# Dilated attention with keys stored by residue and queries copied contiguous

## The reference

```
PATTERNS = ((128, 1), (512, 4), (2048, 16))          # window, dilation d
q, k, v, g_attn, c_h, c_b, c_c, g_conv = split(rmsnorm(x) @ w_in)
q, k = rope(q), rope(k)
for window, d in PATTERNS:
    # positions regrouped by residue mod d: d sequences of 2048 / d positions
    # in blocks of 128: a query sees the keys of its own block and of the one before,
    # at distances 0 .. 128 in its sequence
    s = q . k / 8, masked outside the window
    m = max(s); p = exp(s - m); den = sum(p)
    o_d, lse_d = (p / den) @ v, m + log(den)
w_d = softmax over the three lse_d
attn = sum_d w_d * o_d * silu(g_attn)
x = x + rmsnorm(concat(attn, conv) @ w_out)
```

## Time and profile before

| | |
|---|---|
| median of 3 runs (lowest to highest) | 2533.55 us (2531.64 to 2534.88) |
| the profiled execution, its span | 2524.11 us, 2522.6 us |
| busy in the span: PE, PEld | 2282.0 us (90%), 2068.9 us (82%) |
| DVE, ACT, POOL | 1381.9 us (55%), 819.0 us (32%), 689.7 us (27%) |
| PE matmul L1835 of qkkA, qkqA, x288 | 131.3 us, 456 ns each |
| DVE mask pass L1901, x576 | 185.9 us, 360 ns each |
| DVE rest L1907, x288 | 164.9 us, 572 ns each |
| first and last scores of the dilated stage | 1802.0, 2284.4 us |

### The profile page before, as it was taken

How to read it: one execution, slowest core, us unless ns; L and a number is a source line. 1 busy time by engine, 2 the same in 40 slices (tenths; PEclk the granted TensorE clock), 3 DMA queues, 4 the chain that set the end, 5 groups by cost and what they waited for, 6 DMA issues and landing times.

```text
span 2522.6 us, 42770 instructions
## 1 busy us (share of the span) xinstructions
PE 2282.0 (90%) x16422; PEld 2068.9 (82%) x16422; DVE 1381.9 (55%) x3442; ACT 819.0 (32%) x1910; POOL 689.7 (27%) x658
## 2 busy tenths in 40 slices
PE   6999799988588899599999999999698999996898
PEld 5988799888577688499888888989698888895776
DVE  6513777946699444662365533031386777785321
ACT  4411111111578010242122211000376776774111
POOL 0012021135241798101121211111105444553222
PEclk9999899999899899899999999999898998998999
DMA  4341231124850332332455531211569866964443
GB/s 151 99 111 59 75 96 30 47 83 140 207 145 27 126 123 94 125 110 77 135 184 169 172 126 55 63 36 62 148 146 200 201 166 152 217 181 148 157 140 107
DMA packets 283803, 308.23 MB, mean 122 GB/s; under 512 B 38112, under 2 KB 221280, under 8 KB 280144
## 3 DMA queue, kind: packets, MB, share of 16 engines
q1 hardware_dynamic: 281776, 299.46, 41.4%
q0 software_dynamic: 1680, 5.51, 0.7%
q10 hardware_dynamic: 144, 0.52, 0.1%
HBM read 186.95 MB, written 105.89 MB: 116 GB/s over the span
## 4 chain that ended last, share of the span: by engine, by line
PE 68%; DMA 9%; DVE 9%; issue 5%; POOL 4%; SPq 3%; ACT 1%; ACTq 0%; POOLq 0%; DVEq 0%
PE bank L165 54%; PE bank L1835 4%; DVE acc L694 3%; PE bank L1836 3%; DMA cm<-scr_part 3%; PE bank L1846 3%; PE bank L1864 2%; DMA woR<-in_w_out 2%; PE bank L364 1%; SPq L1955 1%; POOL wol L1201 1%; POOL yo L2113 1%; SPq L1957 1%; PE bank L1269 0%; DMA w2r<-in_w_in 0%
## 5 line engine op out<-in xcount | busy, mean ns | idle before, releaser
L165 PE MATMUL bank<-w1h,xh 128*128 128x256 f32 (+1 forms) x896 | 259.7, 290 | 14.9 <-DVE s1st L684 14.9
L165 PE MATMUL bank<-w1l,xh 128*128 128x256 f32 (+1 forms) x896 | 255.6, 285 | 0.0
L165 PE MATMUL bank<-w1h,xl 128*128 128x256 f32 (+1 forms) x896 | 255.2, 285 | 0.0
L165 PE MATMUL bank<-xh,w2h 128*128 128x512 f32 x640 | 249.0, 389 | 0.0
L165 PE MATMUL bank<-xl,w2h 128*128 128x512 f32 x640 | 249.0, 389 | 0.0
L165 PE MATMUL bank<-xh,w2l 128*128 128x512 f32 x640 | 249.0, 389 | 0.0
L165 PE MATMUL bank<-w2h,xh 128*128 128x256 f32 x768 | 218.5, 284 | 10.3 <-issue 9.0
L165 PE MATMUL bank<-w2l,xh 128*128 128x256 f32 x768 | 217.9, 284 | 0.0
L165 PE MATMUL bank<-w2h,xl 128*128 128x256 f32 x768 | 217.9, 284 | 0.0
L1901 DVE CUSTOM_DVE_ANT_0 s2m<-bank,mask 128x256 f32<-128x256 f32 (+1 forms) x576 | 185.9, 360 | 46.1 <-PE bank L1836 44.5
L694 DVE SCALAR_TENSOR_TENSOR acc<-ain,cw,acc 128x512 f32<-128x512 f32 x240 | 200.1, 835 | 8.9 <-ACT acc L651 1.8
(11 more groups left out here) (273 smaller groups left out, 6017.2 us busy)
## 6 DMA issues: line engine op xcount, KB each, us to landing
scr_part<-ob SPq DMA_DIRECT2D x48, 264.0 KB, 2.8
cm<-scr_part SPq DMA_DIRECT2D x48, 264.0 KB, 4.8
v<-scr_v SPq DMA_DIRECT2D x12, 1040.0 KB, 7.5
w2r<-in_w_in SPq DMA_DIRECT2D x12, 1024.0 KB, 6.8
qr<-qf SPq DMA_DIRECT2D x192, 64.0 KB, 2.0
ax<-in_x SPq DMA_DIRECT2D x16, 512.0 KB, 6.1
xr<-in_x SPq DMA_DIRECT2D x16, 512.0 KB, 4.5
bx<-scr_x SPq DMA_DIRECT2D x16, 512.0 KB, 6.2
```

The source lines that it names most:

```text
L165: ins = nc.tensor.matmul(dst, x, y, start=k == 0 and m == 0, stop=k == n - 1 and m == 2)
```

## The change

1. **Keys by residue.** The rope stage's two split instructions for the 24 key tiles read positions with a stride of 16 and write them in order of their residue mod 16: within each block of 512 positions, 16 runs of 32. The DRAM arrays and the loads stay as they are, only the order of the columns differs.
2. **Queries.** The pair's queries lie in `qn`, both heads in one tile, by position. For d = 1 TensorE still takes them as a contiguous slice. For d = 4 and 16 a new GpSimd instruction ("queries", 96 in all) copies the queries of two units and both heads, 512 columns, to one of six `qs` tiles, contiguous. It is put eight steps ahead of its first unit, ahead of the step's other work, and waits for the pair's loads and for the scores of the unit that used the tile last. The scores of these units wait for it (`g_qs`).
3. **Keys in the matmul** (`keys_of`). For d = 16 runs of 32 columns, for d = 4 runs of 32 in another order, for d = 1 runs of 8. So the scores of d = 4 and 1 leave TensorE with their columns by residue.
4. **The mask pass** puts them back: it reads the bank in its order, reads the mask and writes `s2m` with a stride of 4 elements for d = 4 and of 16 for d = 1. For d = 16 it is unchanged.

```diff
@@ -1426,11 +1426,18 @@
             act_split(N - 2)
             act_split(N - 1)
 
+        def stored(m, x):
+
+            return x[:].rearrange("p (r a) -> p r a", r=16) if tiles[m]["n"] >= 3 else x[:]
+
+        def taken(m, x):
+            return x[:].rearrange("p (a r) -> p r a", r=16) if tiles[m]["n"] >= 3 else x[:]
+
         def act_split(m):
             act.wait_ge(*d_rp.at(3 * m + 3))
             act.wait_ge(*h_out[m % 2].at(16 * (m // 2)))
             act.wait_ge(*d_ql.at(m - 1))
-            nc.scalar.activation(hbuf[m % 2][:], qf[m % 3][:], ACT.Copy).then_inc(*a_qh.up())
+            nc.scalar.activation(stored(m, hbuf[m % 2]), taken(m, qf[m % 3]), ACT.Copy).then_inc(*a_qh.up())
 
         def dve_program():
             for m in range(N):
@@ -1445,7 +1452,7 @@
                 nc.vector.tensor_tensor(q[:], q[:], r[:], ALU.add).then_inc(*d_rp.up())
                 dve.wait_ge(*a_qh.at(m + 1))
                 dve.wait_ge(*l_out[m % 2].at(16 * (m // 2)))
-                nc.vector.scalar_tensor_tensor(lbuf[m % 2][:], q[:], 1.0, f(hbuf[m % 2][:]), ALU.mult, ALU.subtract).then_inc(*d_ql.up())
+                nc.vector.scalar_tensor_tensor(stored(m, lbuf[m % 2]), taken(m, q), 1.0, f(stored(m, hbuf[m % 2])), ALU.mult, ALU.subtract).then_inc(*d_ql.up())
 
         def pool_program():
             for n in range(6):
@@ -1609,7 +1616,8 @@
         ce, cd = sbs("ce", 2, [128, 4, 4, 2], F32, late_scope), sbs("cd", 2, [128, 4, 4, 2], F32, late_scope)
         wp = OutWeights("wp", late_scope, A["w_out_2"], 256, 2, None, None)
         scope = stack().__enter__()
-        qk = [[sb(f"qk{n}{i}", [128, S], FR, scope) for n in ("qA", "qB", "kA", "kB", "lA", "lB")] for i in range(2)]
+        qn, qs = sbs("qn", 2, [128, 2, S], FR, scope), sbs("qs", 6, [128, 2, 2, 128], FR, scope)
+        kk = [[sb(f"qk{n}{i}", [128, S], FR, scope) for n in ("kA", "kB", "lA", "lB")] for i in range(2)]
         vr = sbs("v2", 2, [128, 16, 2 * VW], FH, scope)
         ob = sbs("ob", 4, [128, 4, PW], F32, scope)
         sm, pr = sbs("s2m", 3, [128, 2, 256], F32, scope), sbs("p2r", 4, [128, 2, 256], F32, scope)
@@ -1621,7 +1629,7 @@
         p_s, p_pt, p_o = sem("p_s"), sem("p_pt"), sem("p_o")
         a_ph, a_ex, a_row, a_mix = sem("a_ph"), sem("a_ex"), sem("a_row"), sem("a_mix")
         d_mx, d_pl, d_row, d_min, d_rec, d_mix = (sem("d_" + n) for n in ("mx", "pl", "row", "min", "rec", "mix"))
-        g_zero, g_mix = sem("g_zero"), sem("g_mix")
+        g_zero, g_mix, g_qs = sem("g_zero"), sem("g_mix"), sem("g_qs")
 
         pairs = [(j, d) for j in range(6) for d in (PATTERNS if j < 5 else PATTERNS[::-1])]
         N = 16 * len(pairs)
@@ -1634,6 +1642,11 @@
                 units.append(dict(n=n, j=j, d=d, g=g, r=r, b=b, nk=nk, w=128 * nk, v0=r * nb + b - nk + 1))
 
 
+        copies = [u for u in range(N) if units[u]["d"] > 1 and units[u]["g"] % 2 == 0]
+        for c, u in enumerate(copies):
+            units[u]["copy"] = units[u + 1]["copy"] = c
+
+
         work, later, mixing, n_mix = [], [], [], 0
         mixes, mixed = [], {}
 
@@ -1656,6 +1669,8 @@
         work += [("pair", 0, 4, k) for k in range(10)] + [("values", 0)] + [("pair", 0, 4, k) for k in range(10, 40)]
 
         def step(s):
+            if s + 8 in copies:
+                work.append(("queries", copies.index(s + 8)))
             if s < N:
                 work.append(("scores", s))
             if 0 <= s - 4 < N:
@@ -1816,10 +1831,27 @@
         def mix_dst(m):
             return y2[512 * m["q"]:512 * m["q"] + 512, 128 * m["j"]:128 * m["j"] + 128].rearrange("(t p) c -> p t c", p=128)
 
+        def keys_of(x, k):
+
+            d, r, b, nk = x["d"], x["r"], x["b"], x["nk"]
+            if d == 16:
+                return k[:].rearrange("p (g r a) -> p r g a", g=4, r=16)[:, r]
+            if d == 4:
+                return k[:].rearrange("p (g i r a) -> p r i g a", g=4, i=4, r=4)[:, r, :, b - nk + 1:b + 1]
+            at = [512 * (c // 4) + 8 * (c % 4) for c in (b - nk + 1, b)]
+            return bass.AP(k, at[0], [[S, 128], [32, 16], [at[1] - at[0], nk], [1, 8]] if nk > 1 else [[S, 128], [32, 16], [1, 8]])
+
+        def in_order(x, t):
+
+            return t if x["d"] == 16 else t.rearrange("p (a r) -> p r a", r=16 // x["d"])
+
+        def as_scored(x, t):
+            return t if x["d"] == 16 else t.rearrange("p (r a) -> p r a", r=16 // x["d"])
+
         def pe_unit(item):
             if item[0] == "scores":
                 u, x = item[1], units[item[1]]
-                j, d, w, buf = x["j"], x["d"], x["w"], qk[x["j"] % 2]
+                j, d, w, b, q, buf = x["j"], x["d"], x["w"], x["b"], qn[x["j"] % 2], kk[x["j"] % 2]
                 bank, before = x["s"]
                 if j == 0:
                     for c in range(x["g"] // 4 + 1 if d == 1 else 4):
@@ -1828,12 +1860,13 @@
                     pe.wait_ge(*qk_in[j % 2].at(160 * ((j + 1) // 2)))
                 pe.wait_ge(*g_zero.at(4))
                 pe.wait_ge(*before)
-                q0, k0 = x["r"] + d * 128 * x["b"], x["r"] + d * 128 * (x["b"] - x["nk"] + 1)
-                qc, kc = slice(q0, q0 + d * 127 + 1, d), slice(k0, k0 + d * (w - 1) + 1, d)
+                if d > 1:
+                    pe.wait_ge(*g_qs.at(x["copy"] + 1))
                 for hh in range(2):
                     dst = bank[:, 256 * hh:256 * hh + w]
-                    nc.tensor.matmul(dst, buf[hh][:, qc], buf[2 + hh][:, kc], start=True, stop=False)
-                    ins = nc.tensor.matmul(dst, buf[hh][:, qc], buf[4 + hh][:, kc], start=False, stop=True)
+                    qx = q[:, hh, 128 * b:128 * b + 128] if d == 1 else qs[x["copy"] % 6][:, hh, x["g"] % 2, :]
+                    nc.tensor.matmul(dst, qx, keys_of(x, buf[hh]), start=True, stop=False)
+                    ins = nc.tensor.matmul(dst, qx, keys_of(x, buf[2 + hh]), start=False, stop=True)
                 ins.then_inc(*p_s.up())
             elif item[0] == "turn":
                 u, x = item[1], units[item[1]]
@@ -1898,7 +1931,8 @@
                 dve.wait_ge(*before_row(x))
                 dve.wait_ge(*m_in.at(16))
                 for hh in range(2):
-                    nc.vector.tensor_tensor_reduce(sm[u % 3][:, hh, 0:w], x["s"][0][:, 256 * hh:256 * hh + w], mask2[:, 256 - w:256], 1.0, -NEG,
+                    nc.vector.tensor_tensor_reduce(in_order(x, sm[u % 3][:, hh, 0:w]), as_scored(x, x["s"][0][:, 256 * hh:256 * hh + w]),
+                                                   in_order(x, mask2[:, 256 - w:256]), 1.0, -NEG,
                                                    ALU.add, ALU.min, row[:, 130 + hh:131 + hh]).then_inc(*d_mx.up())
             elif item[0] == "rest":
                 u, x = item[1], units[item[1]]
@@ -1931,7 +1965,21 @@
                     mix_ops(dve, nc.vector, m, part_, d_mix)
 
         def pool_unit(item):
-            if item[0] == "mix":
+            if item[0] == "queries":
+                c, x = item[1], units[copies[item[1]]]
+                j, d, r, b = x["j"], x["d"], x["r"], x["b"]
+                if j == 0:
+                    for i in range(4):
+                        pool.wait_ge(*q0_in[i].at(160))
+                else:
+                    pool.wait_ge(*qk_in[j % 2].at(160 * ((j + 1) // 2)))
+                pool.wait_ge(*g_zero.at(4))
+                if c >= 6:
+                    pool.wait_ge(*p_s.at(copies[c - 6] + 2))
+                src = (qn[j % 2][:].rearrange("p h (b m r) -> p r h b m", b=4, r=4)[:, r, :, b:b + 2] if d == 4 else
+                       qn[j % 2][:].rearrange("p h (m r) -> p h r m", r=16)[:, :, r:r + 2])
+                nc.gpsimd.tensor_copy(qs[c % 6][:], src).then_inc(*g_qs.up())
+            elif item[0] == "mix":
                 m = mixes[item[1]]
                 if m["by"] == "pool" and item[2] in OPS:
                     mix_ops(pool, nc.gpsimd, m, item[2], g_mix)
@@ -1945,16 +1993,16 @@
                 c, hh, part_ = k // 10, k % 10 // 5, k % 5
                 cols = slice(S // parts * c, S // parts * c + S // parts)
                 done = q0_in[c] if parts > 1 else qk_in[j % 2]
-                rows, own, buf = slice(128 * j + 64 * hh, 128 * j + 64 * hh + 64), slice(64 * hh, 64 * hh + 64), qk[j % 2]
+                rows, own, buf = slice(128 * j + 64 * hh, 128 * j + 64 * hh + 64), slice(64 * hh, 64 * hh + 64), kk[j % 2]
                 half = slice(64 * (part_ // 2), 64 * (part_ // 2) + 64)
                 if j >= 2:
                     sp.wait_ge(*p_s.at(48 * (j - 1)))
                 if part_ == 4:
-                    nc.sync.dma_start(f(buf[4 + hh][own, cols]), k2l[rows, cols]).then_inc(*done.up(16))
+                    nc.sync.dma_start(f(buf[2 + hh][own, cols]), k2l[rows, cols]).then_inc(*done.up(16))
                 elif part_ % 2 == 0:
-                    nc.sync.dma_start(f(buf[hh][half, cols]), (q2h, q2l)[hh ^ (part_ // 2)][rows, cols]).then_inc(*done.up(16))
```

(7 more changed lines are left out.)

## The result

The changed kernel takes 2560.11 us (median of 4 runs, 2545.75 to 2560.40), the kernel before, beside it on the same chip, 2532.6 us (2528.42 to 2534.88). The ratio is 1.0097, 95% interval 1.0059 to 1.0134. The forecast was 2509 us with a range from 2485 to 2540.

A forecast was written before the change was run, and what follows sets the result against it. TensorE's strided query loads were taken to pace d = 4 and 16, with VectorE close, DMA and GpSimd limiting later pairs. Gains of 15, 6 and 4 us made 25: 2533.6 - 25 = 2509 us, range 2485 to 2540.

The forecast's parts named there:

- Rope stage, 0 to 0.5 us: Strided ScalarE copies and VectorE subtractions storing keys by residue stay hidden behind busy TensorE: 0 to 0.5 us at stage end.
- Scores: Score matmul steps of d = 4 and 16 fall from 0.22 to 0.11 us; short key runs cost nothing.
- Mask pass, "I take nothing": VectorE's strided mask pass for d = 1 and 4 costs nothing extra; 0.17 us more per wide pass was considered.
- second rival: Strided mask pass is dear: 0.17 us a pass, 26 us, 2535; at double cost per element 2550. Chance 0.18.
- Copies, 0.8 us: Each GpSimd query copy of 128 x 512 takes 0.8 us, between estimates of about 0.6 and 1.04.
- Pairs 1 to 4 up to the third mix, "nothing": d = 4 up to the third mix is DMA-bound; TensorE arrives some 7 us earlier, waits for the same landing: no gain.
- Third mix to next pair: Pairs 1 to 4, from that landing: 16.8 us of GpSimd work, sum 26.0 against 28.0; 1.5 gained per pair, 6 together.
- eight units of 0.95 and 1 us of filling: Pairs 1 to 4, once ScalarE's wait for the fourth mix ends: remaining d = 16 units take 8.6 us.
- Pair 5, "nine units gain 0.4 each": Nine d = 16 units before its first mix gain 3.6 us; GpSimd then 66.1 against 67.4; 4 us gained.
- Pair 0, 15 us: Units 16 to 47, without mixes, go from 52.2 to 37 us: 15 us gained (12 to 17).
- rival 3: GpSimd copies take 1.5 us each: 3.5 us more in each of four pairs, 5 in the last; 2527. Chance 0.06.

The follow-up runs named there:

- mask_psum: Changed kernel with the mask pass walked in natural key order: scores in PSUM read strided, mask and result in SBUF contiguous; ratio 1.0016 to the kernel before.
- six_copies: Kernel before plus GpSimd query copies, natural keys, contiguous mask pass, but only the first six of 96 copies made (wrong output); ratio 0.9888.
- copies_early: Kernel before plus GpSimd query copies queued 14 units ahead into nine tiles, keys natural, mask pass contiguous; ratio 0.9944.
- wide_few: copies_early with 256-column score matmuls in the last eight d = 16 units of pair 4 and first six of pair 5; ratio 0.9933.
- psum_wide: psum_early with copies near a mix moved behind its fourth step, 256-column scores in pair 4's last eight and pair 5's d = 16 units; ratio 1.0021.
- runs_wide: psum_early with 256 columns a score matmul in all d = 16 units; 2508.26 us, ratio 0.991 to the kernel before.
- psum_early: mask_psum with the query copies queued 14 units ahead into nine tiles; ratio 0.9932 to the kernel before.

## Why the prediction was wrong

By its own steps, with lengths from the same cuts (profiled executions; single stretches differ by some us between kernels, d = 4 of pairs 2 and 4 by up to 9):

- *Rope stage, 0 to 0.5 us:* right. Its ScalarE copies went from 632 to 944 ns on average over both kinds, VectorE's subtractions from 692 to 940, and the last stage's first scores start at 1801 us as before.
- *Scores:* right, 0.11 to 0.12 us a step; runs of 8 and 32 read as quickly as a row.
- *Mask pass, "I take nothing":* the first failed step. Measured 0.17 us for a wide pass, the upper bound that I had worked out and set aside, because TensorE's reads bore a stride. That carried one engine's row over to another, and it made the loss in d = 1: of pairs 1 to 4 the d = 1 stretches are 18 us longer than in the kernel before, with the short pass of mask_psum 0.3 us. The Trainium skill (Advanced Engine Details and Errata, section Memory Cachelines) spoke for the second rival with its rule of two accesses to a line. For the SBUF operands the runs agree with it (0.51 us instead of 0.34); the same stride in PSUM showed no price (417 ns with and without). The rival's 26 us were 14 to 20; it had counted nine d = 1 units at the head of a pair, 12 us for the four, where all sixteen grew.
- *Copies, 0.8 us:* mis-sized, 1.09 us, just over the 1.04 that I had as upper bound for the stride. The estimate with the factor of the Trainium skill, GPSIMD Engine Reference, section Performance pitfalls for Q7 kernels, was 0.9 us and too low as well.
- *Pairs 1 to 4 up to the third mix, "nothing":* missed as well. In pair 1 the mix's tile landed 58.5 us after unit 48, against 53.8 in the kernel before, and VectorE stood 7.6 us for it. So the 4.8 us of d = 1 came on top and weren't taken up by that stand; whether the transfers were issued later for it wasn't traced.
- *Third mix to next pair:* GpSimd's 16.8 us were 16.65, by luck, since two errors cancelled: the five copies took 5.3 us instead of 4.0, and the rest 11.4 instead of 12.8, since copies filled the times in which GpSimd waits for ScalarE and VectorE (0.33 and 1.58 us in the kernel before). The failed part, and the second failed step, is the sentence after it, "eight units of 0.95 and 1 us of filling". It took the clock for full, and after TensorE's stand it was at 0.50: they took 1.68 us each; from landing (1932.95) to next pair (1965.33) it was 32.4 us, forecast 26.0 (29.1 before, by the same cut), and eight units of 0.73 us more are 5.8 of these 6.4. For pairs 1 to 4 the forecast was a gain of 6 us; the changed kernel lost 33.4, of which 18 in d = 1, 9 in d = 16 and 6 in d = 4.
- *Pair 5, "nine units gain 0.4 each":* its first sixteen took 26.9 instead of 21.4 us, all at 0.50, though nobody stood there. The clock was brought along from pair 4. The whole pair lost 9.6 us, where 4 were to be gained (its own terms, 3.6 and 1.3, give 4.9).
- *Pair 0, 15 us:* 10.4 (51.7 to 41.4). VectorE at its dear pass was the pace of d = 4 (busy for all of its 25.77 us), but that is the smaller part: with the short pass mask_psum gained 12.1 us, most of what is missing there is in d = 4 too (24.3 us, where VectorE's own sum gave 19.8), and no run shows what holds it.

The sum itself was not bad for what it left out. In six_copies, which makes six copies and has the short mask pass, pair 0 gained 10.3 us, pairs 1 to 4 5.8 and pair 5 4.2, against 15, 6 and 4, and the ratio is 0.9888 where the forecast says 2509 / 2533.6 = 0.990. So the forecast's total is that of a kernel whose costs had no followers; that the two agree so well is in part luck, since the stretches of six_copies add up to 20 us, not 25, and its ratio says 28. Rival 2 named the mask pass at the right price for a pass, but alone it gave 2535; rival 3 priced dear copies at 18 us as GpSimd time. No case had both, and none let TensorE's clock answer to a stand, though the earlier trace rows showed it at 0.79 after the one at 1937 us. There it recovered in d = 4, before d = 16 began.

## What to carry over

When a change makes a stage lighter for TensorE, ask what its clock does there after a stand: here (copies_early) a stand of 2.5 us, at the wrong end of a pair, was followed by 22 units at almost twice their time. A stride that is moved to another engine is priced on that engine and in that memory; here the walk that strides PSUM instead of SBUF takes no longer than one without a stride. And work put on an engine that others wait for in order belongs into that engine's idle time: eight units or fourteen ahead was the difference between a loss and a gain.

## What the hardware did unexpectedly

- TensorE's granted clock, once at 0.50 (1.2 GHz), stayed there through gapless d = 16 units with 128-column score matmuls, for all 26.88 us of pair 5's in ten kernels; with 256-column ones it came back after some 3 to 7 us in three stands (wide_few, psum_wide, runs_wide). The exception is the head of pair 0's d = 16 (psum_early and three others), where the turns and gathers were still those of wide units.
- VectorE: two SBUF operands of 256 fp32 elements at stride 16 take the pass from 0.34 to 0.51 us, one PSUM operand at that stride adds nothing (mask_psum).
- TensorE reads 256 keys at stride 4 in 0.24 us, in runs of 32 in 0.12. The forecast had this difference, 0.12 us for a matmul, as its bound for short runs; the runs cost none of it.
- GpSimd copies 512 fp32 elements with strides of 4 and 16 in 1.09 us.
